# A hybrid attention, mLSTM and PEER layer on one core: second norm inside the output product, eight more u tiles turned beside the queries, first norm in two parts

## The reference, cut to what matters

```python
xn = rmsnorm(xp, norm1_g)                       # 512 prompt frames, the same for 32 sample frames; D = 1024
(aq, ak, av), (mq, mk, mv, ig, lf), mo, ga, gb = _project(xn, w_in, b_in, ml_f_bias)
att = chunk_attention_prompt(aq, ak, av, att_rel_bias)
(Cn, nn_, mn), h = mlstm_prompt(mq, mk, mv, ig, lf)
x = xp + _merge(att, h, mo, ga, gb, w_att_branch, w_ml_branch, w_out)   # ends with merged @ w_out
xn = rmsnorm(x, norm2_g)
q = (xn @ wq).reshape(nb, 8, 2, 64)             # PEER queries
s = einsum('nhpd,hpkd->nhpk', q, sub_keys)      # 128 sub-keys a half; two top-16, then top-16 of the sums
act = gelu(einsum('nhkd,nd->nhk', expert_u[eidx], xn)) ; g = softmax(top scores)
y = rmsnorm(x + einsum('nhk,nhkd->nd', g * act, expert_v[eidx]), final_g)
```

## Time and profile before

| what | value |
|---|---|
| median of 3 runs | 1969.74 us (1967.46 to 1973.33) |
| the profiled execution | 1967.85 us, its span 1966.0 us |
| TensorE busy | 1889.6 us (96%) |
| VectorE busy | 1372.4 us (70%) |
| ScalarE busy | 873.9 us (44%) |
| GpSimd busy | 855.0 us (43%) |
| mean granted TensorE clock | 0.984 |

### The profile page before, as it was taken

The page is one execution under the profiler, slowest core; times in us unless marked ns, Lnnn a source line. Parts: engine busy times, 40 slices in busy tenths (PEclk is TensorE's granted clock), DMA queues, the critical chain, the costliest instruction groups (busy, mean ns, idle before and its releaser), DMA issues. The chain is left out here.

```text
span 1966.0 us, 32250 instructions
## 1 busy us (share of the span) xinstructions
PE 1889.6 (96%) x11529; PEld 1799.4 (92%) x11529; DVE 1372.4 (70%) x2645; ACT 873.9 (44%) x1839; POOL 855.0 (43%) x670
## 2 busy tenths in 40 slices
PE   7999999998989999998999999999999999999998
PEld 6988878887979998998998999999999999999997
DVE  3125746666541898899999877776677777777775
ACT  4021122234131437688888778763333333333333
POOL 4425323331114359699798875751122222222210
PEclk8999999999989999999999999999999999999999
DMA  7632189887711445999999999999799999999982
GB/s 174 117 98 77 53 211 282 270 259 255 179 54 23 137 149 173 278 285 282 289 294 279 283 303 315 320 294 327 257 339 337 352 330 341 350 333 344 351 298 93
DMA packets 325954, 481.08 MB, mean 245 GB/s; under 512 B 37628, under 2 KB 250108, under 8 KB 322468
## 3 DMA queue, kind: packets, MB, share of 16 engines
q1 hardware_dynamic: 287724, 341.63, 56.7%
q0 software_dynamic: 36864, 134.23, 21.2%
q10 hardware_dynamic: 1208, 3.16, 0.4%
HBM read 393.81 MB, written 83.97 MB: 243 GB/s over the span
## 5 line engine op out<-in xcount | busy, mean ns | idle before, releaser
L1493 PE MATMUL ps<-x_high,split_high 128*128 128x416 f32 x1024 | 371.5, 363 | 7.7 <-DVE split_low L1480 5.1
L1493 PE MATMUL ps<-x_high,split_low 128*128 128x416 f32 x1024 | 362.3, 354 | 0.0
L1493 PE MATMUL ps<-x_low,split_high 128*128 128x416 f32 x1024 | 360.5, 352 | 0.0
L2140 PE MATMUL ps<-hid_high,split_high 128*128 128x416 f32 x1024 | 358.9, 350 | 1.5 <-PEq L1707 1.5
L2140 PE MATMUL ps<-hid_low,split_high 128*128 128x416 f32 x1024 | 358.8, 350 | 0.0
L2140 PE MATMUL ps<-hid_high,split_low 128*128 128x416 f32 x1024 | 358.7, 350 | 0.0
L1362 POOL DMA_INDIRECT gathered_rows<-in_peer_v_dram,gathered_index x128 | 135.6, 1059 | 416.9 <-DVE gathered_acc L1399 342.4
L2083 ACT CAST split_high<-area 128x1024 fp32r<-128x1024 f32 x127 | 133.3, 1049 | 383.5 <-PE ps L2140 382.7
L1684 POOL TENSOR_SCALAR area<-iota_row,chosen 128x128 f32<-128x128 f32 x240 | 291.4, 1220 | 2.2
L2111 DVE TENSOR_TENSOR split_low<-area,split_high 128x1024 fp32r<-128x1024 f32 x127 | 155.6, 1225 | 134.4 <-ACT split_high L2083 134.4
L1362 POOL DMA_INDIRECT gathered_rows<-in_peer_u_dram,gathered_index x128 | 152.5, 1192 | 137.7 <-DVE gathered_rows L1377 102.1
(11 more groups left out here) (293 smaller groups left out, 3789.2 us busy)
## 6 DMA issues: line engine op xcount, KB each, us to landing
area<-in_peer_v_dram SPq DMA_DIRECT2D x128, 512.0 KB, 5.6
u_nat<-in_peer_u_dram SPq DMA_DIRECT2D x392, 128.0 KB
routing<-dense SPq DMA_DIRECT2D x26, 1024.0 KB, 6.7
area<-hidden SPq DMA_DIRECT2D x128, 208.0 KB, 7.4
hidden<-gelu_out SPq DMA_DIRECT2D x124, 208.0 KB, 4.6
w_raw<-in_w_in_dram SPq DMA_DIRECT2D x44, 512.0 KB, 6.0
mv_nat<-in_peer_u_dram SPq DMA_DIRECT2D x120, 128.0 KB, 3.6
u_nat<-turned_u SPq DMA_DIRECT2D x30, 512.0 KB
```

The lines of the kernel that those rows point to most:

```text
L1493: ins = self.nc.tensor.matmul(self.k.ps[:, b, 0:N], w[:, b, kk, :], x[:, kk, 0:N], start=(kk == 0 and p == 0), stop=(kk == KD - 1 and p == 2))
L2140: ins = nc.tensor.matmul(ps[:, kk, 0:N], v[:, b, kk * P:(kk + 1) * P], h[:, b, :], start=(n == 0 and p == 0), stop=(n == P - 1 and p == 2))
```

## The change

**Second norm.** The units of the output product are reordered: chunks 0 and 1 for all tiles, then chunks 2 and 3 tile by tile, so that frame tiles are finished one after the other (`ends`). When tile `t` is finished, ScalarE squares it, VectorE takes mean and reciprocal and multiplies by reciprocal and gain (`g2_row`, four instructions of 256 columns, so the gain is no longer in the splits), TensorE turns it between two later units, ScalarE copies (one instruction for a half tile in place of four) and VectorE subtracts. The low parts of the query weights move from GpSimd to VectorE (heads 0 and 1 into the product), and the first two queries run at the end of `merge`. The four DMAs of `g2` go; one of `g2_row` comes.

**Queries.** Queries 2 and 3 come first, then the sub-keys, then the rest. Eight more tiles of u are loaded, turned and stored here (class `Ahead`, the code that ran beside the attention); `AHEAD` is 38.

**First norm.** Statistics of tiles 0 and 1, the splits of tile 0, statistics of tile 2, splits of tiles 1 and 2, the first projection unit, statistics of tiles 3 and 4 and their splits, three more projection units, then the cache and line units. The gain is spread over the partitions by two matmuls and multiplied in by VectorE; a half tile is again split by two instructions. The DMAs of the start are reordered, two of them go to ScalarE's queue.

```diff
-AHEAD = 30
+BESIDE_ATTENTION = 30
+AHEAD = BESIDE_ATTENTION + 8
-LOADS = QUARTERS + 2
+LOADS = 3
...
+QUERY_UNITS = [(0, 0), (1, 0), (0, 1), (1, 1)] + [(m, h) for m in range(2, PH) for h in range(2)]
+QUERIES_AHEAD = 2
+def query(nc, k, pe, i):
+    m, h = QUERY_UNITS[i]
+    pe.wait_ge(k.wq_low_done, m + 1)
+    for kk in range(KD):
+        for p, (w, x) in enumerate(((k.wq_high, k.x_high), (k.wq_high, k.x_low), (k.wq_low, k.x_high))):
+            ins = nc.tensor.matmul(k.ps[:, 4 + i % 4, 0:HALF], w[:, m % 2, kk, :], x[:, kk, h * HALF:(h + 1) * HALF],
+                                   start=(kk == 0 and p == 0), stop=(kk == KD - 1 and p == 2))
+    ins.then_inc(k.q_done, 1)
+def query_weights_high(nc, k, pool, m):
+    if m % 4 == 0:
+        pool.wait_ge(k.wq_loaded[m // 4], 16 * QUARTERS)
+    if m >= 2:
+        pool.wait_ge(k.q_done, 1 + max(i for i, (b, _) in enumerate(QUERY_UNITS) if b == m - 2))
+    nc.gpsimd.tensor_copy(k.wq_high[:, m % 2], query_weights(k, m)).then_inc(k.wq_high_done, 1)
+def query_weights_low(nc, k, dve, m):
+    dve.wait_ge(k.wq_high_done, m + 1)
+    nc.vector.tensor_tensor(k.wq_low[:, m % 2], query_weights(k, m), k.wq_high[:, m % 2], ALU.subtract).then_inc(k.wq_low_done, 1)
...
@@ project @@
-    units = [("xn", (t, g), "vec") for t in range(NT) for g in range(2)]
+    units = [("xn", (t, g), "vec") for t in range(3) for g in range(2)]
...
+        if c == 0:
+            units += new[0:1] + rest_of_x + new[1:4] + cache_and_line + new[4:]
+    STATISTICS_BEFORE = {("xn", (0, 0)): [0, 1], ("xn", (1, 0)): [2], ("xn", (3, 0)): [3, 4]}
@@ project, SP @@
+            load_x(0)
+            sp.dma_start(g1_row, norm1_g).then_inc(g1_loaded, 16)
+            load_x(1)
+            load_x(2)
+            load_tile(0)
+            load_x(3)
+            load_x(4)
+            load_tile(1)
...
@@ project, ScalarE, for each unit @@
+                for t in STATISTICS_BEFORE.get((kind, arg), []):
+                    statistics(t)
                 if kind == "mq" and arg == (0, 0, 0):
-                    act.wait_ge(const_loaded, 144)
+                    act.dma_start(wg_raw[:, :, :], ...).then_inc(wg_loaded, 16)
+                    act.wait_ge(tab_loaded, 48)
@@ project, VectorE, in norm(t), called at the same places @@
+                nc.vector.scalar_tensor_tensor(out=xn[0:r, t, :], in0=x[0:r, t, :], scalar=k.rstd[0:r, t:t + 1],
+                                               in1=ps[0:r, 4:6, :].rearrange("p b n -> p (b n)"), op0=ALU.mult, op1=ALU.mult)
@@ merge @@
+    UNITS = [(i, t) for i in range(2) for t in range(NT)] + [(2, 0), (2, 1), (3, 0), (3, 1)] + [(i, t) for t in range(2, NT) for i in (2, 3)]
+    ends = [UNITS.index((3, t)) for t in range(NT)]
@@ merge, GpSimd, before the cast of the last chunk @@
+                    for m in range(2):
+                        query_weights_high(nc, k, pool, m)
@@ merge, TensorE @@
-            for u in range(OUTS):
-                i, t = divmod(u, NT)
+            for u, (i, t) in enumerate(UNITS):
...
+                if u - 2 in ends[0:4]:
+                    turn(ends.index(u - 2))
+            pe.wait_ge(k.x_low_done, 6)
+            for i in range(QUERIES_AHEAD):
+                pe.wait_ge(out_added, OUTS - 3 + i)
+                query(nc, k, pe, i)
+                if i == 0:
+                    turn(NT - 1)
@@ merge, VectorE, after the add of unit u @@
                 if u in (0, NT + 1, 2 * NT + 1):
                     split_weights(5 + u // NT)
+                if u in (NT + 2, NT + 3):
+                    query_weights_low(nc, k, dve, u - NT - 2)
+                if u in ends:
+                    norm(ends.index(u))
+                if u == ends[2]:
+                    x_low(0)
+                if u > ends[2] and u % 2 == 0:
+                    x_low(1 + (u - ends[2]) // 2)
+            x_low(3)
+            x_low(4)
@@ queries, VectorE @@
+            query_weights_low(nc, k, dve, 2)
             dve.wait_ge(loaded, 16 * LOADS)
...
+            query_weights_low(nc, k, dve, 3)
...
+            later = list(range(BESIDE_ATTENTION, AHEAD))
+            for m in range(4, PH):
+                query_weights_low(nc, k, dve, m)
+                for n in later[2 * (m - 4):2 * (m - 3)]:
+                    ahead.turn(dve, n)
             hidden.split_low(dve, 0)
@@ queries, SP, at the end @@
+            for n in range(BESIDE_ATTENTION, AHEAD):
+                ahead.store(sp, n)
+                if n + 2 < AHEAD:
+                    ahead.load(sp, n + 2)
+            for b in range(2):
+                sp.wait_ge(k.u_stored[b], 16 * AHEAD)
```

More of the change, by code:

```diff
@@ L178, in program @@
             with ExitStack() as now:
-                queries(nc, k, holder(now), hidden, gathered, norm2_g, peer_wq, peer_sub_keys)
+                queries(nc, k, holder(now), hidden, gathered, norm2_g, peer_sub_keys)
             with ExitStack() as now:
@@ L322, in project @@
     bias_masked = sem("bias_masked")
-    units = [("xn", (t, g), "vec") for t in range(NT) for g in range(2)]
-    units += [("cache", s, "act") for s in range(4)]
-    units += [("line", i, "act") for i in range(2)]
+    units = [("xn", (t, g), "vec") for t in range(3) for g in range(2)]
+    rest_of_x = [("xn", (t, g), "vec") for t in range(3, NT) for g in range(2)]
+    cache_and_line = [("cache", s, "act") for s in range(4)] + [("line", i, "act") for i in range(2)]
     sections = [("mq", MQ, mqT, "act"), ("mk", MK, mkT, "vec"), ("mv", MV, mv_nat, "vec"),
@@ L409, in turned_at, with turned_bank @@
     def turned_at(u):
[L411 to L430, removed]
+        return [n for n in range(BESIDE_ATTENTION) if CLEAR + n * (2 * GATE_TILES - CLEAR) // BESIDE_ATTENTION == u]
+    ahead = Ahead(nc, k, ahead_nat, ahead_turned, peer_u)
     def wqk_of(q):
         return pT[:, q % 2, :, :].rearrange("p s n -> p (s n)")
+    STATISTICS_BEFORE = {("xn", (0, 0)): [0, 1], ("xn", (1, 0)): [2], ("xn", (3, 0)): [3, 4]}
+    def turned_bank(u, r):
+        return ps[:, u % BANKS, :].rearrange("p (i n) -> p i n", i=4)[:, :, 0:r]
     with nc.Block() as block:
@@ L863, in _ @@
             pe.wait_ge(vec_const, 1)
+            pe.wait_ge(g1_loaded, 16)
+            for i in range(2):
+                ins = nc.tensor.matmul(ps[:, 4 + i, :], k.ones[0:1, :], g1_row[:, i * 512:(i + 1) * 512], start=True, stop=True)
+            ins.then_inc(g1_spread, 1)
             def turn_back(src, t, b):
@@ L924, in _ @@
                     if arg[0] == 0:
-                        pe.wait_ge(*evicted(last("xn")))
+                        pe.wait_ge(*evicted(units.index(("xn", (2, 1), "vec")) if arg[2] == 0 else last("xn")))
                     ins = section(kind, arg, b)
@@ L1542, in _ @@
             sp.dma_start(g2_row[:, :], norm2_g[0].partition_broadcast(P)).then_inc(loaded, 16)
+            for n in range(BESIDE_ATTENTION, BESIDE_ATTENTION + 2):
+                ahead.load(sp, n)
             for n in range(USLOTS):
@@ L1578, in _ @@
         def _(pe):
[L1579 to L1604 removed]
+            for i in range(QUERIES_AHEAD, 4):
+                query(nc, k, pe, i)
             pe.wait_ge(loaded, 16 * LOADS)
```

297 lines of the change are left out of this document (160 added, 137 removed).

## The result

The forecast was 1961.6 us and faster. Measured were 1975.4 us (median of 20, 1968.8 to 1984.6) against 1970.7 for the kernel before (median of 20): the ratio is 1.0031, 95% interval 1.002 to 1.0042, some 5 to 6 us slower (the medians are 4.7 us apart; the ratio, which is not their quotient, makes it 6.1). The profiled execution took 1980.27 us, 4.9 more than the median; its span is 1978.5, at a mean clock of 0.982.

What follows compares the result with a forecast made beforehand. TensorE was taken to set the time almost everywhere. Terms -14.4, +4.5, +0.7, 0, 0 and +1.1 sum to -8.1 us: profiled 1967.85 becomes 1959.75, and a median 1.89 above gives 1961.6 us; range 1955 to 1968.

Steps and rivals of the forecast that it cites:

- the norm in the product: Second norm, between output product and queries: its 25.1 us hole goes, 10.7 come back on TensorE, net -14.4 us.
- four quarter multiplies: Second norm on VectorE: four multiplies of 256 columns per tile, between 1.3 and some 2.0 us, taken as 1.5.
- the wait before unit 12: Output product: TensorE waits 2.9 us for VectorE's split of chunk 7, plus 1.6 of clock: +4.5 us, bounds 2.9 and 5.5.
- the first norm: Kernel start: first projection unit earlier, second waiting for tiles 3 and 4; net +1.1 us, bounds -3 and +5.
- I get the last split of tile 2 at 16.3: Kernel start: through ScalarE's and VectorE's order, first projection unit starts at 16.3 us, not 26.94.
- chain of tiles 3 and 4: Kernel start: from square to subtraction, two tiles one behind the other, 6.8 us, until 28.4, when the second projection unit starts.
- 18 instructions, 2.0 us: Kernel start: the cache and line units, now after the projection units, cost TensorE 2.0 us at full clock.
- the sub-keys: Queries: their transposition waits for the gain row's DMA, issued 0.4 into the block, 6.5 to landing: +0.7 us (0 to 2).
- Covered, with 2 us to spare: Queries: last u turn about 39 us, store 42, TensorE's last query 44 us after block start; cost 0.
- the search: Search stage: routing waits come five steps earlier, not smaller: 0; bounds 9.9 us saved or 7 lost.
- rival 2: Search: VectorE's relief shows if the sorts' end holds the routing; half to all of 9.9 us gained, 1954 us; chance 0.10.
- rival 3: Search: denser sort pieces make dots late, so routing waits grow; slower, about 1977 us; chance 0.08.

Runs made afterwards that it cites:

- line-early: Changed kernel with the cache and line units turned before the second projection unit, not after the fourth: 1970.3 us, ratio 1.0002 to the kernel before.
- split early: Changed kernel with VectorE's split of chunk 7 one product unit earlier, behind the add of unit 10: 1971.5 us, ratio 1.0013 to the kernel before.
- kernel with the turns first: Changed kernel with line, statistics, chunk 7 split and sub-keys moved, each pair of u tiles turned ahead of VectorE's query-weight split: 1960.5 us, ratio 0.9951.
- the last two kernels: Changed kernel without eight u tiles, four moves, ScalarE taking out queries 0 to 3 before copying sub-keys: 1951.4 us; same with the previous first norm: 1957.2 us.
- old first norm: Changed kernel with the first norm of the kernel before, all else as changed: 1965.6 us, ratio 0.9970 to the kernel before.
- statistics early: Changed kernel with squares, roots and scaling of tiles 3 and 4 ahead of the first projection unit's eviction: 1968.6 us, ratio 1.0002 to the kernel before.
- no eight tiles: Changed kernel without the eight more u tiles, which are turned in the search again: 1972.8 us, ratio 1.0009 to the kernel before.
- sub-keys later: Changed kernel with the transposition of the sub-keys after the sixth query, not the fourth: 1976.7 us, ratio 1.0032 to the kernel before.

## Why the prediction was wrong, point by point

**Right: the norm in the product.** -14.4 forecast, -13.9 in the trace. The norm was covered: no turn waited for it. Of the four quarter multiplies, put between 1.3 and some 2.0 us and taken as 1.5, the trace has 1.67 a tile (568.20 to 569.87 for tile 0); whether strided reads are the reason no run shows.

**Right in kind: the wait before unit 12.** Forecast 4.5, of which 1.6 for the clock; the trace has +2.7, the wait alone. Three other kernels lost the clock there and kept it after unit 0 (last section). Undoing the wait took 2.7 us out of the trace.

**Wrong: the first norm, +1.1 forecast, +5.4 in the trace.** The step that failed is "I get the last split of tile 2 at 16.3": it ended at 18.96. The sum went through ScalarE's and VectorE's order and left out that VectorE's multiply of tile 0 waits for the spread gain, 2.38 us (8.55, above). The chain of tiles 3 and 4 was well sized (6.8 forecast, from 24.21 to 31.29 are 7.1) and started late by about as much, so that the second unit came at 31.29 and not at 28.4: 2.9 of the 4.3 us. That it is this wait which passes through is read off the trace; no run took it out. Most of the rest are two sizes: the second unit took 5.1 us and not 4.3 (31.29 to 36.42), and the cache and line units 2.4 and not 2.0 (42.45 to 44.83).

**Wrong: nothing was put down for the weights, +4.6.** Of the moved cache and line units I priced TensorE's "18 instructions, 2.0 us" and not who waits for them: VectorE's line, then SyncE's first piece, then the weight tiles queued behind. The line-early kernel shows it: with these units moved up, the wait of 4.32 us is gone.

**Wrong: the sub-keys, +0.7 forecast (0 to 2), +4.1.** The place was named. The term that was mis-sized is the gain row's DMA: it landed 8.5 us after the block began (604.9 - 596.4) and not 6.5 + 0.4, and the 2.26 us cost clock as well (0.50 from 606 to 609), for which I had put nothing. Why it was late is open. The loads of the u tiles stand beside it, and without them the wait was 0.76 us; but with them split early has a wait of 1.01, and over the kernels here this DMA takes 6.4 to 8.1 us with these loads and 5.8 to 7.7 without.

**Wrong: "Covered, with 2 us to spare", 0 forecast, +2.0 and the clock after it.** The last turn was to come 39 us after the block began and came at 45.4. The first one starts at 19.5, behind a split that waits for GpSimd, and the pace is (641.85 - 615.94) / 7 = 3.7 us a tile, the last ones waiting for their loads. In the kernel with the turns first the boundary is mended and the splits are late: with two buffers and one VectorE neither order had room for eight tiles. Fewer tiles or more buffers were not tried.

**Right: the search, 0.** From the first to the last product it took 732.5 us after and 724.1 before. But over all kernels here with the eight tiles it took 720.1 to 732.5 (mean 726.1 of seven), without them 724.1 to 729.1 (mean 725.5 of five). The 8.4 us of this pair are spread; the mean difference is 0.7, with a standard error of about 1.8, and neither rival 2 (VectorE's relief, 5 to 10 us) nor rival 3 (later dots, 8 us and more) shows. Eight transpositions less on VectorE brought nothing that can be seen.

Together: 4.3 (first norm) + 4.6 (weights) + 3.4 (sub-keys) + 2.0 (boundary) + 0.7 (search) - 1.8 (unit 12) + 0.5 (norm) - 0.6 (mLSTM to branches) = 13.1 of the 14.2 us between the forecast of -8.1 and the measured +6.1 (0.31% of 1970); it comes to +5.0, close to the 4.7 us between the medians. The result lies nearest to the time of rival 3 (1977), by none of its mechanism. The range ended at 1968 because I had bounded the terms that I saw. The weights and the wait for the spread gain were not among them, and the boundary's 1 to 3 us were named but stood in no bound.

Not settled: how much of the 5.8 us between the last two kernels is more than the start; what made the gain row's DMA late; and what decides at which of two equal waits the clock falls.

## What to carry to other kernels

When units of work are moved in one engine's order, follow what they produce to its last reader on every queue: here six short units, moved by four, delayed a weight stream by way of VectorE and SyncE. An operation that stands behind an eviction, though its data is there, is the first thing to look for in a pipelined prologue; one entry in a table moved it, and the second projection unit started 4.4 us earlier. Background work in a short block has to be costed with the wait at the block's end, where its last store counts, not its busy time.

## What the runs showed of the hardware

Two waits of equal length did not cost the same. Six kernels have both, 2.7 us before unit 0 and 2.7 us before unit 12, 37 to 38.5 us apart. In three of them (changed, old first norm, line early) the granted clock was 0.50 after the first and 1.00 after the second, as the windows 524 to 527 and 563 to 566 above show; in the other three (statistics early, no eight tiles, sub-keys later) it was 1.00 after the first and 0.50 after the second, as in the windows 520 to 523 and 557 to 562 of the statistics-early kernel. None had it after both. That there is a second wait does not decide it: of the six kernels with the wait before unit 0 alone, five show 0.50 after it, and split early shows 1.00 from 526 to 530.

The granted 1.00 of the first 22 us does not fit the pace of the matmuls. In the window from 19 to 22 the changed kernel makes 13 matmuls, in that from 36 to 42 it makes 50, both at 1.00; so the first ran at half the pace. The statistics-early kernel makes 15 in the same first window and shows 0.50. The prediction's choice, to go by the pace and against the row, was right: the first unit took from 19.06 to 23.83, 4.8 us. By the Trainium skill ("TensorE: Matmul & The Clock Gate", Part 1) the throttled clock is the default and activity releases it; these windows agree.
